# Norm statistics as four columns instead of a 128x512 tile, in a three-block transformer kernel

## The chip, the cores and the metric

One Trainium2 chip, one of its cores. The metric is the device time of one execution of the whole program, in microseconds (us). The core has five engines that run their own instruction streams and meet at semaphores: PE (TensorE, matrix products; PEld is its loading of weights), DVE (VectorE), ACT (ScalarE), POOL (GpSimd) and SP (SyncE, which here only starts transfers).

## The reference, cut to what matters

512 tokens of 2048 features go through two hybrid layers and then a second block. All norms divide by a root mean square over the features, one number per token:

```python
def rms_norm(x, w, eps=1e-6):
    return x * rsqrt(mean(x * x, axis=-1) + eps) * w

# layer l = 0, 1
proj = rms_norm(x, pre_w) @ w_in                  # norm x0, x1
qc   = rms_norm(c_q, q_norm_w) @ w_uq             # norm cq0, cq1 (512 features)
kvc  = rms_norm(c_kv, kv_norm_w) @ w_ukv          # norm ckv0, ckv1 (512 features)
x    = x + rms_norm(y @ w_out, post_w)            # norm post0, post1
# second block
h    = ... rmsnorm(x, norm_gain) @ w_in_2 ...     # norm x2
h    = h + (h @ w_out_2 part) + (p @ w_ple) * sigmoid(h @ w_ple_gate)
out  = rmsnorm(h, final_gain)                     # norm fin
```

That is ten norms. Everything is in float32.

## The kernel before

**Layout.** Activations lie feature-major: a tile `tiles[:, kt]` is 128 features by 512 tokens, and `kt` counts 16 of them. A number per token therefore runs along the free axis and must be the same in all 128 partitions before it can multiply a tile.

**Products.** A weight or activation is split into a high part (rounded to the type `fp32r`) and a low part, and a product is three matmuls of 128x512 (lines 1657 to 1659). Weights come in units of four 128x256 blocks through a ring of four slots: SP loads `w_raw` (L393), ACT casts it to `w_hi` (L531, in `split_one`) as soon as PE has finished with the slot, POOL subtracts to make `w_lo` in two halves (L518), and PE waits for `wlo_done`. One unit is 24 matmuls. PE's order is written out by hand: `plan_units` numbers the units and each engine's code walks through them. At `first_pairs` (the first eight units of a block that starts with a norm) PE takes tile after tile, 12 matmuls each, as `act_lo[:, kt]` becomes ready.

**A norm.** Squares are summed over tiles into one 128x512 tile. For x0, x1 and x2, ACT writes 16 squares into `wide` and DVE adds them at the end in four wide operations (`sum_squares`, L1089: 4096, 2048, 1024 and 512 columns). For cq and ckv DVE squares and adds (`square_sum`), for post and fin it does so in the loop that takes the products out of PSUM (L1315 to L1318, L1638 to L1642). PE multiplies the sum with a 128x128 matrix of ones (`ones_product`, L1726), which leaves the token's sum in all partitions, 128x512. `rms` (L937 to L939) then does on 128x512: scale and add eps on DVE, root on ACT (`root`, L557), reciprocal on DVE. For cq and ckv the result lies in `rstd_lat`, for the others in `rstd`. The norm of x is applied late: the products are taken from PSUM with a multiplication by `rstd` (L908). PE transposes `rstd` (L1881) and DVE copies four columns of it to `rcol` (L1196), which a later product needs per token.

**Where the norms stand on PE.** x0 and x1: the ones product after the second of four `ckr` units; the units of `ckv` that follow need PSUM banks that DVE frees by taking the first products with `rstd`. cq: after the third `ckv` unit. ckv: after the second unit of `bg1`. post0 and post1: after the last unit of `wo`; nothing is queued on PE until DVE has made the first tile of the next block (`tiles*rstd` L1330, gain and residual L1331, low part L916; ACT does high part L745 and square L747 between). x2: right after its `first_pairs`. fin: last; then 16 scaled tiles (L1647) and the stores (L504).

## Time and profile before

| | us |
|---|---|
| median of three runs | 2897.19 |
| lowest run | 2896.59 |
| the profiled execution, in all | 2892.89 |
| its span, first to last instruction | 2891.1 |
| PE busy (share of the span) | 2733.6 (95%) |
| DVE busy | 1514.5 (52%) |
| ACT busy | 848.4 (29%) |
| POOL busy | 1202.4 (42%) |

Times in the trace are microseconds from the start of the span; a row of the timeline gives start and length. Matmuls are pipelined: a row's length overlaps the next row's start, so the cost of one is the distance between starts. An `x2` behind a row merges two instructions; one float32 product is two of them on PE, one `fp32r` product is one. The clock column is the granted TensorE clock: 1.00 is 2.4 GHz, 0.50 is 1.2 GHz.

### The profile page before, as it was taken

How to read it: one execution, taken by the hardware profiler on the slowest of the kernel's cores; microseconds unless marked ns; L12 is line 12 of the kernel's file. 1: busy time of each engine (PE TensorE's matmuls, PEld its weight loads, DVE VectorE, ACT ScalarE, POOL GpSimd, SP SyncE). 2: the span in 40 equal slices, each digit the busy share in tenths (PEclk: the TensorE clock that was granted, in tenths of full speed). 3: DMA queues.
4: the chain of work that ended last, by engine and by line, in shares of the span. 5: the costliest groups of instructions: out<-in, count | busy, mean ns of one | idle time of the engine just before them, and what ended most of it. 6: DMA issues, size and time to landing. Idle time of an engine off the chain costs nothing.

```text
span 2891.1 us, 34107 instructions
## 1 busy us (share of the span) xinstructions
PE 2733.6 (95%) x12638; PEld 2152.5 (74%) x12638; DVE 1514.5 (52%) x2088; ACT 848.4 (29%) x1374; POOL 1202.4 (42%) x860
## 2 busy tenths in 40 slices
PE   7999999999998999999999999798999988999996
PEld 5777877877786787887777787676666667788885
DVE  4653146478425644227548732938898683211524
ACT  4233214225313332213315422312222233322321
POOL 5452442442443653343352344423332254455542
PEclk9999999999999999999999999898999989999998
DMA  4332332321433332232231333312211322432331
GB/s 153 97 116 66 95 89 61 89 77 45 167 94 97 118 105 81 87 95 73 71 90 52 142 101 98 140 59 80 66 51 59 124 80 85 151 98 89 108 95 73
DMA packets 246196, 268.65 MB, mean 93 GB/s; under 512 B 20544, under 2 KB 237248, under 8 KB 243648
## 3 DMA queue, kind: packets, MB, share of 16 engines
q1 hardware_dynamic: 240512, 222.33, 25.9%
q10 hardware_dynamic: 5568, 44.74, 4.0%
q8 instruction: 78, 1.28, 0.2%
q14 instruction: 38, 0.31, 0.0%
HBM read 246.06 MB, written 20.97 MB: 92 GB/s over the span
## 4 chain that ended last, share of the span: by engine, by line
issue 55%; POOL 31%; PE 12%; DVE 1%; POOLq 1%; ACT 0%; DVEq 0%
POOL w_lo L518 31%; PE gemm_ps L1657 4%; PE gemm_ps L1658 4%; PE gemm_ps L1659 4%; DVE tiles L1647 0%; POOLq L516 0%; POOLq L514 0%; PE to_ps L1658 0%; PE to_ps L1657 0%; PE s_ps L1658 0%; PE s_ps L1657 0%; PE s_ps L1659 0%; PE to_ps L1659 0%; DVE rstd L939 0%; PE to_ps L1726 0%
## 5 line engine op out<-in xcount | busy, mean ns | idle before, releaser
L518 POOL TENSOR_TENSOR w_lo<-w_raw,w_hi 128x512 fp32r<-128x512 f32 x856 | 1202.2, 1427 | 1644.7 <-ACT w_hi L531 1644.6
L1657 PE MATMUL gemm_ps<-act_hi,w_hi 128*128 128x512 f32 x2848 | 1142.7, 401 | 75.7 <-DVE mask_b L1099 21.2
L1658 PE MATMUL gemm_ps<-act_lo,w_hi 128*128 128x512 f32 x2848 | 1118.5, 393 | 0.0
L1659 PE MATMUL gemm_ps<-act_hi,w_lo 128*128 128x512 f32 x2848 | 1118.2, 393 | 0.0
L531 ACT CAST w_hi<-w_raw 128x1024 fp32r<-128x1024 f32 x428 | 447.9, 1050 | 1500.4 <-PE gemm_ps L1659 1308.9
L1657 PEld LDWEIGHTS gemm_ps<-act_hi,w_hi 128*128 128x128 f32 x2848 | 540.7, 190 | 224.4 <-issue 87.4
L1659 PEld LDWEIGHTS gemm_ps<-act_hi,w_lo 128*128 128x128 f32 x2848 | 540.3, 190 | 116.0
L1658 PEld LDWEIGHTS gemm_ps<-act_lo,w_hi 128*128 128x128 f32 x2848 | 541.1, 190 | 111.9 <-issue 4.3
L908 DVE TENSOR_TENSOR tiles<-gemm_ps,rstd 128x512 f32<-128x512 f32 (+1 forms) x58 | 39.3, 689 | 281.3 <-PE gemm_ps L1659 278.0
L1315 DVE COPY tiles<-gemm_ps 128x512 f32 x32 | 22.2, 693 | 221.1 <-PE gemm_ps L1659 220.7
L1608 DVE TENSOR_TENSOR tiles<-gemm_ps,att 128x512 f32<-128x512 f32 x16 | 11.0, 690 | 141.5 <-PE gemm_ps L1659 141.5
L984 DVE TENSOR_TENSOR att<-to_ps,sin_t 128x512 f32<-128x512 f32 x40 | 27.6, 689 | 79.9 <-PE to_ps L1754 79.9
L1022 DVE TENSOR_REDUCE small<-s_ps 128x1 f32<-128x128 f32 (+5 forms) x48 | 26.7, 557 | 81.0 <-PE s_ps L1798 80.6
L1638 DVE SCALAR_TENSOR_TENSOR att<-att 128x512 f32 x16 | 14.7, 919 | 101.8 <-ACT att L885 88.0
L584 ACT ACTIVATE att<-att,small 128x256 f32<-128x256 f32 (+1 forms) x128 | 60.1, 473 | 19.4 <-DVE small L1018 19.4
L1813 PE MATMUL to_ps<-cst,att 128*128 128x128 f32 x384 | 57.6, 272 | 6.8 <-ACT att L606 3.6
L1813 PEld LDWEIGHTS to_ps<-cst,att 128*128 128x128 f32 x384 | 46.5, 139 | 18.3 <-issue 4.4
L916 DVE SCALAR_TENSOR_TENSOR act_lo<-tiles,col,act_hi 128x512 fp32r<-128x512 f32 x48 | 45.8, 972 | 22.9 <-ACT act_hi L657 22.5
L1657 PE MATMUL gemm_ps<-sub_hi,w_hi 128*128 128x512 f32 x96 | 42.2, 439 | 14.7 <-DVE tiles L1507 14.4
L995 DVE TENSOR_TENSOR tiles<-tiles,att 128x512 f32<-128x512 f32 x36 | 54.0, 1500 | 1.2
L591 ACT ACTIVATE att<-s_ps,small 128x128 f32<-128x128 f32 (+1 forms) x64 | 31.8, 500 | 69.5 <-DVE small L1023 69.5
L908 DVE TENSOR_TENSOR att<-gemm_ps,rstd 128x512 f32<-128x512 f32 x32 | 21.6, 688 | 55.6 <-PE gemm_ps L1659 55.5
(380 smaller groups left out, 3166.8 us busy)
## 6 DMA issues: line engine op xcount, KB each, us to landing
w_raw<-in_w_in_dram SPq DMA_DIRECT2D x248, 512.0 KB
w_raw<-in_w_out_dram SPq DMA_DIRECT2D x96, 512.0 KB
w_raw<-in_w_ple_gate_dram SPq DMA_DIRECT2D x32, 512.0 KB
gate_scratch<-att ACTq DMA_DIRECT2D x16, 512.0 KB, 2.6
x_scratch<-tiles ACTq DMA_DIRECT2D x4, 2048.0 KB, 7.9
att<-x_scratch ACTq DMA_DIRECT2D x2, 4096.0 KB, 13.2
w_raw<-in_w_glu_dram SPq DMA_DIRECT2D x32, 256.0 KB
tiles<-in_x_dram ACTq DMA_DIRECT2D x4, 1024.0 KB, 10.7
```

The costliest lines, as they stand in the source:

```text
L518: ins = pool.tensor_tensor(w_lo[:, s, k:k + 2], w_raw[:, s, k:k + 2], w_hi[:, s, k:k + 2].bitcast(F32), ALU.subtract)
L531: act.copy(w_hi[:, slot], w_raw[:, slot]).then_inc(whi_done, 1)
L584: act.activation(v, v, ACT.Exp, bias=sm[:, 4 + j:5 + j], scale=SCALE[br], accum_out=sm[:, 8 + j:9 + j])
L591: last = act.activation(prob[n % 3][:, c * 512:c * 512 + nk], src, ACT.Exp, bias=sm[:, 4 + c:5 + c], scale=SCALE[br], accum_out=sm[:, 8 + ...
L908: tt(dst, ps[:, f, :], scale[:], ALU.mult).then_inc(bank_taken[f], 1)
L916: ins = stt(act_lo[:, kt], tiles[:, kt], scale, act_hi[:, kt].bitcast(F32), ALU.mult, ALU.subtract)
L984: tt(sq[:, n % 2], t_ps[:, n % 2, :], sin_t[:], ALU.mult).then_inc(rope_read, 1)
L995: tt(t, t, sq[:, n % 2], ALU.add).then_inc(roped, 1)
L1657: pe.matmul(ps, left_hi, right_hi, start=first, stop=False, skip_group_check=True)
L1658: pe.matmul(ps, left_hi, right_lo, start=False, stop=False, skip_group_check=True)
L1659: return pe.matmul(ps, left_lo, right_hi, start=False, stop=last, skip_group_check=True)
L1813: mm = pe.transpose(t_ps[:, a, k * 128:(k + 1) * 128], prob[n % 3][:, a * 512 + k * 128:a * 512 + (k + 1) * 128], ident)
```

## The change

**The statistic.** `ones_product` is replaced by two steps. `norm_cols` multiplies, for each of four token blocks, the 128x128 block of squares (as the weights) with four columns of ones: the sum comes out as a column, one token per partition. `rms` then does its arithmetic on 128x4 (L950 to L953), writes four 128x128 diagonals (L955), and `norm_rows` (L1764) multiplies ones with the 128x512 of diagonals, which gives the row form in PSUM, read from there by who needs it; for x norms it is copied to `rstd` (L959). The transposes of `rstd` and the copy to `rcol` go.

**The sums of squares.** `sum_squares` is replaced by `partial_sum`: 11 additions of 128x512, one after most tiles, which leave five partial sums (tiles 0, 4, 8, 12 and 15) that `norm_cols` adds up in PSUM. For post and fin the last two tiles are squared on ACT instead of DVE, straight from PSUM at post, and enter as two more partial sums.

**Casts.** L531 becomes two casts of 128x512, each with its semaphore step, and POOL waits for each half.

**Moves.** The products for lambda stand at the start instead of behind the sine tables; ACT casts two units fewer ahead of the roots of x0 and x1.

```diff
-                act.copy(w_hi[:, slot], w_raw[:, slot]).then_inc(whi_done, 1)
+                for k in range(0, UK, 2):
+                    act.copy(w_hi[:, slot, k:k + 2], w_raw[:, slot, k:k + 2]).then_inc(whi_done, 1)
...
-            split_until(14)
+            split_until(12)
             root("x0")
...
                 through(("wo", l), 32)
+                for f in range(2):
+                    act.wait_ge(mm_done, unit_end(("wo", l), 31) + f + 1)
+                    if f:
+                        act.wait_ge(ssq_in, NORMS[f"post{l}"] + 1)
+                    act.activation(last_sqs[f], gemm_ps[:, f, :], ACT.Square).then_inc(last_sq, 1)
                 root(f"post{l}")
...
             def rms(norm, n_feat):
-                to = rstd_lat if norm[0] == "c" else rstd[:]
-                dve.wait_ge(ssq_out, SSQ[norm])
-                ts(to, o_ps[:, 0, :], 1.0 / n_feat, EPS, ALU.mult, ALU.add).then_inc(var_done, 1)
-                dve.wait_ge(sqrt_done, NORMS[norm] + 1)
-                dve.reciprocal(to, to).then_inc(rstd_done, 1)
-                dve.wait_ge(rstd_done, NORMS[norm] + 1)
+                i, c = NORMS[norm], norm_col(norm)
+                dve.wait_ge(ssq_out, i + 1)
+                ts(c, o_ps[:, 0, 0:16].rearrange("p (t n) -> p t n", n=4)[:, :, 0], 1.0 / n_feat, EPS,
+                   ALU.mult, ALU.add).then_inc(var_done, 1)
+                dve.wait_ge(sqrt_done, i + 1)
+                own.link(dve.reciprocal(c, c))
+                for t in range(TT):
+                    ins = ts(diag[:, t * 128:(t + 1) * 128], ident, norm_col(norm, t, 1), None, ALU.mult)
+                ins.then_inc(diag_done, 1)
+                dve.wait_ge(rows_done, i + 1)
+                if norm[0] == "x":
+                    dve.tensor_copy(rstd[:], o_ps[:, 0, :]).then_inc(rstd_done, 1)
+                    dve.wait_ge(rstd_done, int(norm[1:]) + 1)
...
-            def sum_squares(v):
-                dve.wait_ge(sq_done, KT * (v + 1))
-                for n in (8, 4, 2, 1):
-                    ins = tt(wide_flat[:, 0:n * T], wide_flat[:, 0:n * T], wide_flat[:, n * T:2 * n * T], ALU.add)
+            def partial_sum(v, kt):
+                if kt % 4 and kt < KT - 1:
+                    dve.wait_ge(sq_done, KT * v + kt + 1)
+                    ins = tt(wide[:, kt - kt % 4], wide[:, kt - kt % 4], wide[:, kt], ALU.add)
...
-            def ones_product(norm, squares=sq[:, 0]):
-                pe.wait_ge(ssq_in, SSQ[norm])
-                pe.matmul(o_ps[:, 0, :], ones[:], squares, start=True, stop=True).then_inc(ssq_out, 1)
+            def norm_cols(norm, squares):
+                pe.wait_ge(ssq_in, NORMS[norm] + 1)
+                for t in range(TT):
+                    for i, s in enumerate(squares):
+                        mm = pe.matmul(o_ps[:, 0, 4 * t:4 * t + 4], s[:, t * 128:(t + 1) * 128], ones[:, 0:4],
+                                       start=i == 0, stop=i == len(squares) - 1)
+                mm.then_inc(ssq_out, 1)
+            def norm_rows(norm):
+                pe.wait_ge(diag_done, NORMS[norm] + 1)
+                pe.matmul(o_ps[:, 0, :], ones[:], diag, start=True, stop=True).then_inc(rows_done, 1)
+            def x_cols(v):
+                pe.wait_ge(sq_done, KT * (v + 1))
+                norm_cols(f"x{v}", [wide[:, k] for k in (0, 4, 8, 12, 15)])
...
                 first_pairs(("cq", l), f"x{l}")
+                x_cols(l)
...
-                    if j == 1:
-                        ones_product(f"x{l}", wide[:, 0])
+                    if j == 0:
+                        norm_rows(f"x{l}")
...
                 one_pair(("ckv", l), 1, 0)
-                pe.wait_ge(rstd_done, NORMS[f"x{l}"] + 1)
-                for t in range(TT):
-                    mm = pe.transpose(t_ps[:, 0, t * 128:(t + 1) * 128], rstd[:, t * 128:(t + 1) * 128], ident)
-                mm.then_inc(rcol_tp, 1)
+                norm_rows(f"cq{l}")
```

Not shown: cq's columns stand where its ones product stood; ckv's too, with its rows one unit later; post, x2 and fin have columns and rows next to each other.

**PE after the first eight units of a layer, x0.** Before, the ones product came 24 matmuls into `ckr` (the fragment shows its neighbours):

```order
L1659 MATMUL to_ps<-act_hi,w_lo 128x512
L1726 MATMUL to_ps<-att,ones 128x512
L1657 MATMUL to_ps<-act_hi,w_hi 128x512
```

Of the change, the seam between `first_pairs` (s_ps) and the first `ckr` unit (to_ps), cut after its third matmul:

```order
L1687 MATMUL s_ps<-act_hi,w_lo 128x512
L1757 MATMUL to_ps<-ones,att 128x4 x20
L1685 MATMUL to_ps<-act_hi,w_hi 128x512
L1686 MATMUL to_ps<-act_lo,w_hi 128x512
L1687 MATMUL to_ps<-act_hi,w_lo 128x512
```

One product became 20 with 128 weights and four columns each, ahead of the unit, and the rows (L1764) follow 12 matmuls later.

**DVE after the norm post0.** These rows make the tiles of layer 1; before, three per tile:

```order
L1330 TENSOR_TENSOR tiles<-tiles,rstd 128x512
L1331 SCALAR_TENSOR_TENSOR tiles<-tiles,col,att 128x512
L916 SCALAR_TENSOR_TENSOR act_lo<-tiles,col,act_hi 128x512
L1330 TENSOR_TENSOR tiles<-tiles,rstd 128x512
L1331 SCALAR_TENSOR_TENSOR tiles<-tiles,col,att 128x512
L916 SCALAR_TENSOR_TENSOR act_lo<-tiles,col,act_hi 128x512
```

Of the change, from the fourth tile on:

```order
L1352 TENSOR_TENSOR tiles<-tiles,to_ps 128x512
L1353 SCALAR_TENSOR_TENSOR tiles<-tiles,col,att 128x512
L929 SCALAR_TENSOR_TENSOR act_lo<-tiles,col,act_hi 128x512
L1109 TENSOR_TENSOR att<-att 128x512
L1352 TENSOR_TENSOR tiles<-tiles,to_ps 128x512
L1353 SCALAR_TENSOR_TENSOR tiles<-tiles,col,att 128x512
L929 SCALAR_TENSOR_TENSOR act_lo<-tiles,col,act_hi 128x512
```

The additions L1109 that stood behind the last tile as four wide ones stand between the tiles now.

## Rows read from the trace of the kernel before

**Rows 1.** Timeline, PE: start us, length us, engine, line, operation, count, [idle before <-releaser]

```profile
72.65 1.02 PE L1726 MATMUL to_ps<-att,ones 128*128 128x512 f32 x2
...
73.75 0.40 PE L1658 MATMUL to_ps<-act_lo,w_hi 128*128 128x512 f32 x1
...
80.16 0.47 PE L1657 MATMUL gemm_ps<-act_hi,w_hi 128*128 128x512 f32 x1 [1.03 <-POOL w_lo L518]
...
108.14 0.40 PE L1659 MATMUL gemm_ps<-act_hi,w_lo 128*128 128x512 f32 x1
108.37 0.60 PE L1881 MATMUL to_ps<-cst,rstd 128*128 128x128 f32 x4
108.73 0.48 PE L1657 MATMUL gemm_ps<-act_hi,w_hi 128*128 128x512 f32 x1
```

**Rows 2.** Timeline around norm post0, PE and DVE

```profile
909.41 1.15 PE L1726 MATMUL to_ps<-att,ones 128*128 128x512 f32 x2 [3.50 <-DVEq L1324]
...
911.98 3.35 DVE L939 RECIPROCAL rstd<-rstd 128x512 f32<-128x512 f32 x1 [0.69 <-ACT rstd L557]
...
915.37 0.69 DVE L1330 TENSOR_TENSOR tiles<-tiles,rstd 128x512 f32<-128x512 f32 x1
...
919.05 0.77 PE L1657 MATMUL gemm_ps<-act_hi,w_hi 128*128 128x512 f32 x1 [8.49 <-DVE act_lo L916]
```

**Rows 3.** Stretch table, PE: busy (count), granted clock, DMA share, GB/s

```profile
912.00:914.00 2.00, 0.00 (x0) 0.50 0.68 236
```

**Rows 4.** Timeline through the tiles of x1, and norm x1: DVE and PE

```profile
933.18 1.79 DVE L1330 TENSOR_TENSOR tiles<-tiles,rstd 128x512 f32<-128x512 f32 x1
...
956.80 11.64 DVE L1089 TENSOR_TENSOR att<-att 128x4096 f32<-128x4096 f32 x4
...
964.78 0.39 PE L1659 MATMUL s_ps<-act_hi,w_lo 128*128 128x512 f32 x1
...
981.51 1.29 DVE L908 TENSOR_TENSOR tiles<-gemm_ps,rstd 128x512 f32<-128x512 f32 x2 [3.14 <-DMA x_scratch<-tiles]
...
982.34 0.76 PE L1657 MATMUL gemm_ps<-act_hi,w_hi 128*128 128x512 f32 x1 [3.37 <-DVE tiles L908]
```

**Rows 5.** Timeline, norm x2 on PE

```profile
1862.62 2.02 PE L1726 MATMUL to_ps<-att,ones 128*128 128x512 f32 x2 [3.26 <-DVE att L1089]
1871.49 0.76 PE L1657 MATMUL gemm_ps<-act_hi,w_hi 128*128 128x512 f32 x1 [6.84 <-DVE tiles L908]
```

**Rows 6.** Timeline, norm fin: PE and DVE

```profile
2869.41 1.89 PE L1726 MATMUL to_ps<-cos_t,ones 128*128 128x512 f32 x2 [4.40 <-DVEq L1644]
...
2876.12 10.69 DVE L1647 SCALAR_TENSOR_TENSOR tiles<-tiles,col,rstd 128x512 f32<-128x512 f32 x16
```

**Rows 7.** Timeline at the lambda product: PEld, PE, DVE

```profile
130.75 0.50 PEld L1888 LDWEIGHTS to_ps<-col,ones 64*128 64x128 f32 x2 [5.85 <-DVE col L1119]
130.75 0.59 PE L1888 MATMUL to_ps<-col,ones 64*128 64x4 f32 x2 [5.43 <-DVE col L1119]
...
130.83 1.27 DVE L908 TENSOR_TENSOR tiles<-gemm_ps,rstd 128x512 f32<-128x512 f32 x2
...
131.65 0.77 PE L1657 MATMUL gemm_ps<-sub_hi,w_hi 128*128 128x512 f32 x1 [0.31 <-DVE tiles L908]
```

**Rows 8.** By line, L2000: min/median/max ns, first and last start us

```profile
L2000 PE MATMUL to_ps<-att,tiles x128: 196/196/217, 1936.7 to 1938.0; 128*32 128x32 f32 x128
```

**Rows 9.** Timeline, first matmul, norm cq0 and a small copy, PE and DVE

```profile
21.18 0.77 PE L1657 MATMUL gemm_ps<-act_hi,w_hi 128*128 128x512 f32 x1 [21.18 <-DVE mask_b L1099]
...
108.50 1.42 DVE L947 SCALAR_TENSOR_TENSOR tiles<-tiles,col,att 128x512 f32<-128x512 f32 x2
...
113.86 0.16 DVE L1196 COPY col<-to_ps 128x4 f32<-128x4 f32 x1
```

**Rows 10.** Page, costliest groups: xcount | busy us, mean ns | idle before, releaser

```profile
L518 POOL TENSOR_TENSOR w_lo<-w_raw,w_hi 128x512 fp32r<-128x512 f32 x856 | 1202.2, 1427 | 1644.7 <-ACT w_hi L531 1644.6
L531 ACT CAST w_hi<-w_raw 128x1024 fp32r<-128x1024 f32 x428 | 447.9, 1050 | 1500.4 <-PE gemm_ps L1659 1308.9
```

More of the change, by code:

```diff
@@ L338, in build_program @@
         NORMS = {k: i for i, k in enumerate(order)}
+        last_sqs = [rstd[:], sq[:, 1]]
         VERS, total = {}, 0
@@ L344, in build_program, with norm_col @@
             total += n_tiles
-        SSQ = {"x0": 1, "cq0": 2, "ckv0": 3, "post0": 4, "x1": 5, "cq1": 6, "ckv1": 7, "post1": 8, "x2": 9, "fin": 10}
+        def norm_col(norm, t=0, n=4):
+            return C("rcol" if norm[0] == "x" else "ncol", t, n)
         def unit_end(key, units):
@@ L555, in root @@
                 act.wait_ge(var_done, NORMS[norm] + 1)
-                to = rstd_lat if norm[0] == "c" else rstd[:]
-                act.activation(to, to, ACT.Sqrt).then_inc(sqrt_done, 1)
+                act.activation(norm_col(norm), norm_col(norm), ACT.Sqrt).then_inc(sqrt_done, 1)
             def split_act(version, kt, src, scale):
@@ L889, in _ @@
                 act.activation(sq[:, f], gemm_ps[:, f, :], ACT.Tanh, scale=0.5).then_inc(bank_taken[f], 1)
+            for f in range(2):
+                act.wait_ge(fin_in, f + 1)
+                act.activation((rstd, sin_t)[f][:], tiles[:, 14 + f], ACT.Square).then_inc(last_sq, 1)
             root("fin")
@@ L946, in latent @@
                     if kt < 4:
-                        stt(tiles[:, first + kt], tiles[:, first + kt], C(gain, 4 * l + kt), rstd_lat,
+                        stt(tiles[:, first + kt], tiles[:, first + kt], C(gain, 4 * l + kt), o_ps[:, 0, :],
                             ALU.mult, ALU.mult).then_inc(lat_in, 1)
@@ L1093, in sum_squares @@
                         ins.then_inc(ssq_in, 1)
-            for kt in range(KT):
+            tt(C("prod", 0, 2)[0:64], C("lam4", 0, 2)[0:64], C("lam4", 2, 2)[0:64], ALU.mult)
+            tt(C("prod", 2, 2)[0:64], C("lam4", 4, 2)[0:64], C("lam4", 6, 2)[0:64], ALU.mult).then_inc(lam_sum, 1)
+            for kt in range(KT + 1):
                 if kt == 4:
@@ L1308, in _ @@
                 own.link(dve.memset(sq[:, 0], 0.0))
-                for first, count in ((0, 2), (2, 2), (4, 4)):
+                for first, count in ((0, 2), (2, 2), (4, 3)):
                     with dve.Fori(0, count) as i:
@@ L1324, in _ @@
                 dve.nop().then_inc(ssq_in, 1)
+                for f in range(2):
+                    dve.wait_ge(last_sq, 2 * l + f + 1)
+                    take(f, tiles[:, 14 + f], None)
                 rms(f"post{l}", D)
@@ L1329, in _ @@
                     if kt < KT:
-                        own.link(tt(tiles[:, kt], tiles[:, kt], rstd[:], ALU.mult))
+                        if kt >= 14:
+                            dve.wait_ge(bank_taken[kt % 2], at[("wo", l)][1] + 9)
+                        own.link(tt(tiles[:, kt], tiles[:, kt], o_ps[:, 0, :], ALU.mult))
                         stt(tiles[:, kt], tiles[:, kt], C("post", 16 * l + kt), wide[:, kt],
@@ L1642, in _ @@
                     own.link(tt(cos_t[:], cos_t[:], sin_t[:], ALU.add))
-            own.leave(8)
+            own.leave(7)
             dve.nop().then_inc(ssq_in, 1)
+            for f in range(2):
+                w, t = wide[:, 14 + f], tiles[:, 14 + f]
+                dve.wait_ge(bank_taken[f], 7 + (at[("pleg", 0)][1] + 2))
+                stt(w, sq[:, f], 1.0, w, ALU.add, ALU.mult).then_inc(pleg_tanh, 1)
+                dve.wait_ge(pleg_tanh, 14 + f + 3)
+                stt(t, w, 0.5, t, ALU.mult, ALU.add).then_inc(fin_in, 1)
             rms("fin", D)
             for kt in range(KT):
-                stt(tiles[:, kt], tiles[:, kt], C("fgain", kt), rstd[:], ALU.mult, ALU.mult).then_inc(fin_scaled, 1)
+                stt(tiles[:, kt], tiles[:, kt], C("fgain", kt), o_ps[:, 0, :], ALU.mult, ALU.mult).then_inc(fin_scaled, 1)
         @block.tensor
@@ L1902, in _ @@
                     if j == 1:
-                        ones_product(f"ckv{l}")
+                        norm_cols(f"ckv{l}", [sq[:, 0]])
+                    elif j == 2:
+                        norm_rows(f"ckv{l}")
                 if l:
@@ L1974, in _ @@
                 pairs(("wo", l), 8, first=1, order=Y_UNITS)
-                ones_product(f"post{l}")
+                pe.wait_ge(last_sq, 2 * l + 2)
+                norm_cols(f"post{l}", [sq[:, 0]] + last_sqs)
+                norm_rows(f"post{l}")
             first_pairs(("si", 0), f"x{LAYERS}")
-            ones_product(f"x{LAYERS}", wide[:, 0])
+            x_cols(LAYERS)
+            norm_rows(f"x{LAYERS}")
             def state_rows(v):
@@ L2106, in _ @@
             pairs(("pleg", 0), 8, first=1)
-            ones_product("fin", cos_t[:])
+            pe.wait_ge(last_sq, 2 * LAYERS + 2)
+            norm_cols("fin", [cos_t[:], rstd[:], sin_t[:]])
+            norm_rows("fin")
 _INS = ["x", "positions", "w_in", "w_uq", "w_ukv", "w_out", "p_2", "w_in_2", "w_pool_2", "w_glu_2", "w_out_2",
```

49 lines of the change are left out of this document (22 added, 27 removed).

## The prediction

> **What bounds the kernel now.** I read the page first: PE is busy for 95% of the span, so time comes only from what PE executes and from the 157 us in which it stands still. Then I followed its stops along the timeline; those that a norm causes are few. The reader is to see, in this order: after post0 PE stops for 3.50 us, does the ones product and stops for 8.49 us, of which the reciprocal alone is 3.35 [rows 2]; the same pattern returns at post1. At x2 it stops for 3.26 and 6.84 us [rows 5], at x1 for 3.37 us, behind DVE which waited for the store of x [rows 4], at x0 for 1.03 us [rows 1], and at fin 4.40 us before the ones product, with the output scaled only from 2876.12 on [rows 6]. The lambda product is released 5.43 us late, but the unit behind it also needs the banks that DVE frees at 130.83, so that stop ends with DVE's queue and not with the product [rows 7]. Everywhere else PE is fed: cq0, cq1, ckv0 and ckv1 lie almost wholly under weight units.
>
> So the change can win only at post0, post1, x2 and fin. At x0, x1, cq and ckv it adds work to an engine that is full.
>
> **The price of a column product.** The trace has no float32 product of 128 weight columns with four moving ones, except the lambda product (64 rows): two instructions, weight loads of 0.50 us together, matmuls of 0.59 us together, at half clock [rows 7]. From lengths and ends the two loads start 0.17 us apart, the two matmuls 0.22. At full clock that is 0.085 to 0.11 us for an instruction. A float32 block with 128 moving columns fits it: four transposes take 0.36 us, 0.09 each [rows 1]. Bound below: 128 instructions with 32 weight columns each start within 1.3 us, 0.011 each [rows 8]; bound above: 0.22, half clock [rows 7]. I take 0.09, since the form is that of rows 7. The change has three norms x with 20 products, three (post, fin) with 12 and four (cq, ckv) with 4: 112 products, 224 instructions, 20.2 us of PE time. A whole ones product costs 0.87 us at full clock (72.65 to 73.75 less one matmul of 0.23, the distance of 108.14 to 108.37) and some 2.0 us at half clock [rows 1, 5]; rows cost the same.
>
> Here a page speaks against my price. The Trainium skill, TensorE: Matmul & The Clock Gate, section Back-to-back issue gap, gives about 60 cycles, 25 ns, for a matmul with 1 to 64 moving columns. By that the 224 would be an estimated 5.6 us. No row here has this form at full clock, so the page is not refuted; the sum below stands on rows 7.
>
> **The small steps.** Between columns and diagonals stand a scale, a root, a reciprocal and four diagonals of 128x128. A copy of 128x4 out of PSUM took 0.16 us [rows 9]; seven such steps and the hops between engines make 1.5 us, where 128x512 took 0.69 + 0.63 + 3.35 and hops. The root's table load stays ahead of its wait at x0 and lies under the column products at post and fin: nothing.
>
> **Term by term, plus is slower.**
>
> Start: the first matmul waits for `mask_b` [rows 9]; now the sums of tiles 1 and 2 stand ahead of it on DVE, 0.7 us each, half of one covered. +0.9. PE has no stop behind it that would absorb it until x0.
>
> x0: 40 x 0.09 = 3.6 for the columns; rows for the ones product, even; the stop of 1.03 goes, since `rstd` is ready earlier than `ckv` begins. +2.6.
>
> cq0: rows are queued behind the unit that ended at 108.37. They end 1.05 later, 109.4, where DVE began the latents at 108.50 [rows 1, 9]: +0.9. Columns 8 x 0.09 = 0.7 for 0.87: -0.15. The lambda operations and the copy to `rcol` leave DVE's queue: -0.2. All of it passes through the sine tables into the take at 130.83. +0.6.
>
> ckv0: columns -0.15, rows +0.87. +0.7.
>
> post0 and x1: the last matmul ends at 905.92 (909.41 less 3.50). ACT does a cast (1.05, now in halves [rows 10]) and two squares of about 0.55: 908.2. Columns 24 x 0.09 and drain: 910.6. Small steps: 912.1. The clock is at 0.50 by 912 [rows 3], so rows take 2.0: DVE starts the tiles at 914.1 instead of 915.37. But each tile then costs DVE more. Before, nine tiles took 17.8 us, 2.05 each after the first, and while POOL runs an operation takes 1.79 instead of 0.69 [rows 4], twice for four operations, 8.7 us in all. Low part 12 now comes at 914.1 + 3.5 + 12 x 2.05 + 8 sums x 0.73 + 8.7 = 956.7, later than PE would want it, and PE has four tiles of 2.72 left: 967.6, where it ended its first pairs at 965.0. Then columns 3.6, rows 0.9, four `ckr` units 10.9: 983.0. Before, PE went on at 982.34, after a stop that left it at half clock (0.76 for a matmul that is 0.40 long otherwise), some 1.3 us for the first six: 983.6 [rows 4]. The four wide sums of 11.64 us vanish, but PE never waited for their end here. The store of x is issued two casts earlier and no longer ends last. -0.6.
>
> cq1 and ckv1: as in layer 0, but rows are now on PE's path and the transposes (0.36 [rows 1]) go: +0.35 and +0.7. +1.0.
>
> post1 and x2: the first pairs end 2.7 later, as at x1: 1862.05. Columns 3.8 with drain, small steps 1.5, rows at half clock 2.0, copy to `rstd` 0.7, first take 0.8: 1870.8 against 1871.49 [rows 5]. -0.7.
>
> fin: last matmul 2865.01. Two tanh, two DVE steps of 0.75, square: 2868.0. Columns 2.4, small steps 1.5, rows 1.9: scaling starts at 2873.8 instead of 2876.12 [rows 6]. -2.3. The 10.69 us behind it read PSUM instead of SBUF, at the same length as other products out of PSUM (L908, 0.64 each in a pair [rows 4]).
>
> Halved casts: POOL gets its first half 0.5 us earlier, and ACT pays an instruction more per unit. PE waits for neither: a unit lasts 5.4 us, POOL needs 2.85 of it and is released by ACT, ACT by PE [rows 10]. 0, cover 2.5 us per unit.
>
> Sum: 0.9 + 2.6 + 0.6 + 0.7 - 0.6 + 1.0 - 0.7 - 2.3 = +2.2 us on the profiled execution of 2892.89: 2895.1. The median of the runs stands 4.3 above that execution, so the forecast for a median is 2899.
>
> **The rivals.**
>
> *Columns are cheap.* If the weight loads hide behind each other, an instruction costs 0.05 or less. Speaks for it: rows 8. Against: those are quarter-width tiles. At 0.05 the sum is 2.2 - 224 x 0.04 = -6.8, median 2890; at the page's 25 ns (same section of the Trainium skill) it would be an estimated 2885. At the bound of rows 8, -15.6: 2881.5.
>
> *The columns leave the clock low* (the other side, slower). Products of four columns hardly fill the array, and the clock was at 0.50 after a stretch with little more than a ones product in it [rows 3]. If it falls during x0's and x1's columns too, these double (3.6 each, also at x2), rows cost 1.1 more and the next dozen matmuls pay 0.2 each: about +6 at each of two sites and +3.6 at x2, +16 in all: 2915. It decides from the point where one x norm shows a clock below 0.7 in the 5 us after its columns. Against it: the ones product among the weight units of x0 left the matmul at 73.75 at its 0.40 [rows 1], and a column stretch is not much longer.
>
> *DVE becomes the bound in the first pairs.* Margin per tile: 2.72 for PE, 2.05 + 0.55 for DVE. If the added sums meet POOL more often than the old ones, each pays 1.1 more; five of them per x norm, two norms: +11, 2910. For it: every DVE operation beside POOL is stretched [rows 4].
>
> *The halves starve the ring.* Needs 2.5 us more per unit; 0.14 us for each of 428 units would already be 58 us, 2%. Nothing in rows 10 points there.
>
> **How the numbers follow.** Forecast 0.45, its own range 2895 to 2904 (0.08 to 0.11 per instruction, start and cq0 half a microsecond either way). Cheap columns 0.22, 2882 to 2894. Low clock 0.13, 2905 to 2916. DVE bound 0.17, 2904 to 2912. Others 0.03. Range for 8 in 10: 2888 to 2910; the bound above for the price, +29 us, would need half clock everywhere and is left out. A measurement of this kernel tells 2% (58 us) from no change, and no case but the last reaches it: faster 0.01, same 0.98, slower 0.01.
>
> **What would show each step.** Distance between column products 0.09 us, x columns 3.6 us long. No stop before `ckv` at x0 and x1. First pairs of x1 and si ending 48 to 50 us after the diagonals' use begins, with PE stopping for DVE between tiles 8 and 12. Reciprocals no longer above 0.2 us. Scaling at fin starting 8.8 us after the last `pleg` matmul, 11.1 before. The forecast is wrong if the columns cost under 0.06 or over 0.12, or if the clock at x0 falls.

## The result, and the profile after

The changed kernel takes 2902.01 us, the median of 20 runs (2897.18 to 2907.39), where the kernel before took 2894.16 us in 20 runs beside it. The ratio is 1.0027 with a 95% interval of 1.0021 to 1.0033, so 7.8 us (6 to 10) slower, and within 2%. One of the 20 runs of the kernel before, at 5244.23 us, stands far off the others; without it their median would be 2893.41. I had forecast +2.2 us, and 2899 on a base of 2897.19 us. The profiled executions exaggerate the difference. The one of the kernel before (2892.89 us) stands 1.3 us below its median and the one of the changed kernel (2906.21 us) 4.2 above its own, so that the spans, 2891.1 and 2904.4 us, differ by 13.3.

Part 1 of the page after, the busy time, share and instructions of each engine:

```profile
PE 2765.3 (95%) x12854; PEld 2182.2 (75%) x12854; DVE 1475.0 (51%) x2138; ACT 885.7 (30%) x1808; POOL 1183.9 (41%) x860
```

The first matmul, from PE's timeline (start and length in us, engine, line, operation, out<-in; in brackets the idle time ahead and what ended it), and DVE's timeline just before it. It answers the 21.18 of [rows 9]:

```profile
24.50 0.77 PE L1685 MATMUL gemm_ps<-act_hi,w_hi 128*128 128x512 f32 x1 [24.50 <-DVE mask_b L1121]
...
19.90 0.68 DVE L1109 TENSOR_TENSOR att<-att 128x512 f32<-128x512 f32 x1
...
21.29 0.68 DVE L1109 TENSOR_TENSOR att<-att 128x512 f32<-128x512 f32 x1
22.01 1.17 DVE L1120 CAST ident_b<-cst 128x128 bf16<-128x128 f32 x1
23.10 1.30 DVE L1121 CAST mask_b<-cst 128x128 bf16<-128x128 f32 x1
```

Two sums of 0.68 us stand ahead of the casts, and the casts, which now fall beside POOL's work, are 1.17 and 1.30 long instead of 0.21. That second part I had not counted.

The norm x0 on PE, columns (L1757) and rows (L1764), and on DVE scale, reciprocal, diagonals and copy (answering [rows 1]):

```profile
69.81 6.14 PE L1757 MATMUL to_ps<-ones,att 128*128 128x4 f32 x40
75.81 0.78 PE L1685 MATMUL to_ps<-act_hi,w_hi 128*128 128x512 f32 x1
76.39 0.63 PE L1686 MATMUL to_ps<-act_lo,w_hi 128*128 128x512 f32 x1
...
80.24 1.02 PE L1764 MATMUL to_ps<-att,ones 128*128 128x512 f32 x2
...
75.99 0.16 DVE L950 TENSOR_SCALAR col<-to_ps 128x4 f32<-128x4 f32 x1 [29.75 <-PE to_ps L1757]
76.42 0.18 DVE L953 RECIPROCAL col<-col 128x4 f32<-128x4 f32 x1 [0.27 <-ACT col L562]
76.64 0.87 DVE L955 TENSOR_SCALAR att<-cst,col 128x128 f32<-128x128 f32 x4
81.30 0.69 DVE L959 COPY rstd<-to_ps 128x512 f32<-128x512 f32 x1 [3.79 <-PE to_ps L1764]
```

And PE's table by stretches of x0 (busy us and instructions, granted clock, DMA share, GB/s), the third stretch being the first matmuls behind the columns; below them the 5 us behind the columns of x0, x1 and x2:

```profile
69.80:72.40 2.60, 2.60 (x25) 1.00 0.02 6
72.40:75.80 3.40, 3.40 (x18) 0.50 0.57 159
75.80:79.20 3.40, 3.40 (x9) 0.50 0.79 189
79.20:82.00 2.80, 2.80 (x11) 0.99 0.14 46
...
75.80:80.80 5.00, 5.00 (x16) 0.65 0.62 154
979.20:984.20 5.00, 5.00 (x17) 0.66 0.99 300
1874.20:1879.20 5.00, 2.08 (x2) 0.50 1.02 321
```

The first 24 column instructions start 0.111 us apart. Then the granted clock falls to 0.50 (1.2 GHz, from 2.4) although PE never stands still, the rest start 0.213 apart, and the eight matmuls behind them are 0.54 to 0.78 long instead of 0.39. At x2 the clock fell in the kernel before too, as its ones product began, behind a stop of 3.26 us [rows 5].

The norm post0 (answering [rows 2]), first and last row of the 24 column instructions, rows, and restart; and the end of fin (answering [rows 6]):

```profile
916.45 0.38 PE L1757 MATMUL to_ps<-ones,att 128*128 128x4 f32 x2 [2.21 <-ACT att L750]
...
918.93 0.57 PE L1757 MATMUL to_ps<-ones,att 128*128 128x4 f32 x2
921.11 2.07 PE L1764 MATMUL to_ps<-att,ones 128*128 128x512 f32 x2 [1.61 <-DVE att L955]
926.89 0.77 PE L1685 MATMUL gemm_ps<-act_hi,w_hi 128*128 128x512 f32 x1 [3.71 <-DVE act_lo L929]
...
2889.49 10.62 DVE L1675 SCALAR_TENSOR_TENSOR tiles<-tiles,col,to_ps 128x512 f32<-128x512 f32 x16 [2.17 <-PE to_ps L1764]
```

**Where the time went.** I cut PE's timeline at the same places in each trace: ends of first pairs, the start of `ckv`, the restart at uq0 (the first weight unit that needs the norm cq0), the last matmul of `wo` (a layer's output product, ahead of post) and of `pleg` (the last product, ahead of fin). The second block starts at its unit `si`. "Again" is a second trace of the changed kernel. Lengths in us:

| stretch | before | after | again | forecast | found |
|---|---|---|---|---|---|
| to the first matmul, and x0's first pairs | 67.20 | 69.81 | 70.47 | +0.9 | +2.6, +3.3 |
| x0: columns, rows, `ckr` | 12.95 | 19.47 | 19.49 | +2.6 | +6.5 |
| cq0: `ckv` to uq0's restart | 51.49 | 52.33 | 52.33 | +0.6 | +0.8 |
| ckv0 and the attention of layer 0 | 774.27 | 772.64 | 770.75 | +0.7 | -1.6, -3.5 |
| post0 | 13.13 | 12.65 | 13.68 | | |
| first pairs of x1 | 45.96 | 47.91 | 47.90 | | |
| x1 to `ckv`; with the two above | 17.33 | 17.88 | 19.48 | -0.6 | +2.0, +4.6 |
| cq1, ckv1 and the attention of layer 1 | 817.73 | 815.23 | 815.18 | +1.0 | -2.5 |
| post1, first pairs, x2 | 71.40 | 72.74 | 72.88 | -0.7 | +1.3, +1.5 |
| second block, si to fin | 993.53 | 999.16 | 998.96 | 0 | +5.6, +5.4 |
| fin to the end | 26.08 | 24.59 | 24.79 | -2.3 | -1.5, -1.3 |

The same cut by kind of time, up to PE's last instruction: PE's idle time, half of the busy time at a granted clock of 0.50, and the rest, which is work at full clock:

| kernel | idle | lost to the clock | work |
|---|---|---|---|
| before | 137.7 | 46.1 | 2687.5 |
| changed | 124.2 | 57.1 | 2708.2 |
| changed, again | 127.4 | 54.3 | 2709.3 |
| one summed tile (e1) | 136.8 | 47.3 | 2700.1 |
| and diagonals on ACT (e6) | 133.4 | 48.1 | 2699.0 |
| new scheme at post and fin alone (e8) | 122.0 | 52.5 | 2692.9 |
| and the store of x first (e9) | 118.1 | 56.7 | 2693.8 |

So the change does what it says: 13.5 us of stops are gone. It pays 20.7 us of PE work for them, and another 11.0 us at half clock. The second trace has 10.3, 21.8 and 8.2: the work is the same within about 1 us, the split between stops and clock is not. The row of e9 is that kernel's slowest run (2885.46 us, where its median is 2878.18).

### The profile page after: what moved, and what is told of

Its sections match the earlier page's. It is cut to its first block and busy times, and to the rows that moved or that the text cites. A ratio compares the mean times of both kernels' runs of the same rounds, so it can differ in the third digit from the quotient of the medians.

```text
span 2904.4 us, 35445 instructions
## 1 busy us (share of the span) xinstructions
PE 2765.3 (95%) x12854; PEld 2182.2 (75%) x12854; DVE 1475.0 (51%) x2138; ACT 885.7 (30%) x1808; POOL 1183.9 (41%) x860
## 5 line engine op out<-in xcount | busy, mean ns | idle before, releaser
L524 POOL TENSOR_TENSOR w_lo<-w_raw,w_hi 128x512 fp32r<-128x512 f32 x856 | 1183.7, 1406 | 1677.9 <-ACT w_hi L537 1677.8
L537 ACT CAST w_hi<-w_raw 128x512 fp32r<-128x512 f32 x856 | 486.0, 618 | 1480.5 <-PE gemm_ps L1687 1289.0
L921 DVE TENSOR_TENSOR tiles<-gemm_ps,rstd 128x512 f32<-128x512 f32 (+1 forms) x58 | 39.3, 688 | 285.0 <-PE gemm_ps L1687 284.8
L919 DVE COPY tiles<-gemm_ps 128x512 f32<-128x512 f32 x24 | 16.1, 682 | 70.5 <-ACT rstd L750 38.4
```

Source lines behind the costliest of these rows:

```text
L524: ins = pool.tensor_tensor(w_lo[:, s, k], w_raw[:, s, k], w_hi[:, s, k].bitcast(F32), ALU.subtract)
L537: act.copy(w_hi[:, slot, k:k + 2], w_raw[:, slot, k:k + 2]).then_inc(whi_done, 1)
L921: tt(dst, ps[:, f, :], scale[:], ALU.mult).then_inc(bank_taken[f], 1)
```

## The experiments

Ratios are those to the kernel before on the same chip; the changed kernel's was 1.0027, and 1.0030 (1.0018 to 1.0043) when it was run again. The intervals are about 2.5 to 3.8 us wide to either side, which bounds what a single comparison can settle. One microsecond is 0.00035.

**One summed tile (e1).** Is it the number of columns?

```
-                if kt % 4 and kt < KT - 1:
+                if kt:
...
-                    ins = tt(wide[:, kt - kt % 4], wide[:, kt - kt % 4], wide[:, kt], ALU.add)
+                    ins = tt(wide[:, 0], wide[:, 0], wide[:, kt], ALU.add)
...
-                norm_cols(f"x{v}", [wide[:, k] for k in (0, 4, 8, 12, 15)])
+                norm_cols(f"x{v}", [wide[:, 0]])
```

> DVE adds all sixteen squares of x0, x1 and x2 into one tile (15 additions instead of 11), so that each x norm has 4 column products (8 instructions) instead of 20 (40). Theory 'the columns and the clock that they lose': in the changed kernel the 40 instructions take 6.0, 4.4 and 5.9 us at x0, x1 and x2, 0.111 each at full clock and 0.213 at half, and 7 to 8 ckr matmuls behind them are 0.2 us longer each. With 8 instructions the clock stays at full: -5.1 -1.6 at x0, -3.5 -1.6 at x1, -5.0 +0.7 (one more addition behind the last square) at x2, about -16 us: 2886. Theory 'only the instructions count' (the clock falls anyhow): 96 x 0.111 to 0.15, -10.7 to -14 us less nothing. Rival 'DVE is the bound in the first pairs': four more additions of 0.73 to 1.8 us per x norm are late for the last low parts, so PE's stop of 1.1 us for act_lo at x1 and x2 grows by 3 to 7 us each: gain only 2 to 9 us, 2893 to 2900.

Measured: 1.0031 (1.0018 to 1.0044), no gain. The timelines at x1 of PE, DVE and POOL:

```profile
976.38 0.95 PE L1758 MATMUL to_ps<-ones,att 128*128 128x4 f32 x8
982.99 1.12 PE L1765 MATMUL to_ps<-att,ones 128*128 128x512 f32 x2 [2.78 <-DVE att L955]
...
977.37 0.16 DVE L950 TENSOR_SCALAR col<-to_ps 128x4 f32<-128x4 f32 x1 [1.84 <-PE to_ps L1758]
977.92 0.18 DVE L953 RECIPROCAL col<-col 128x4 f32<-128x4 f32 x1 [0.38 <-ACT col L562]
978.13 4.81 DVE L955 TENSOR_SCALAR att<-cst,col 128x128 f32<-128x128 f32 x4
...
974.94 9.22 POOL L524 TENSOR_TENSOR w_lo<-w_raw,w_hi 128x512 fp32r<-128x512 f32 x7
```

POOL at x0 in the changed kernel, whose diagonals stand at 76.64 to 77.51:

```profile
73.08 1.26 POOL L524 TENSOR_TENSOR w_lo<-w_raw,w_hi 128x512 fp32r<-128x512 f32 x1
```

The eight columns take 0.95 us as expected, and 8 us of work and 10 us of lost clock are gone (7 against the second trace). But the idle time rose by 12.6: the four diagonals take 4.81 us instead of 0.87, and PE waits 3.42, 2.78 and 5.63 us for them at x0, x1 and x2. No theory had this. In the changed kernel POOL ended at 74.34 and had nothing further until the diagonals were done. That the long columns had kept PE from freeing weight slots is my reading of it; what the traces show is that behind short columns the diagonals run beside POOL. At x0 the clock fell in e1 as well, at 77.3 us behind that stop, so that x0 took 19.31 us against 19.47. And the first pairs of x1 and x2 took 49.4 us instead of 47.9: the four more sums per norm do come late, as the third theory had it, for 1.5 us each.

**Diagonals on ACT (e6).** Tests just that; everything else is as in e1.

```
                 act.activation(norm_col(norm), norm_col(norm), ACT.Sqrt).then_inc(sqrt_done, 1)
+                act.wait_ge(recip_done, NORMS[norm] + 1)
+                for t in range(TT):
+                    ins = act.activation(diag[:, t * 128:(t + 1) * 128], ident, ACT.Copy, scale=norm_col(norm, t, 1))
+                ins.then_inc(diag_done, 1)
```

> As the kernel with one tile (e1), and ACT writes the four diagonals (Copy with the column as its scale) instead of DVE, at every norm. Theory 'DVE's diagonals beside POOL ate the gain of e1': there PE waited 3.4, 2.8 and 5.6 us for them at x0, x1 and x2, the four of them being 4.8 to 5.3 us long. On ACT they take about 4 x 0.25 us, whatever POOL does: the stops fall by 3.4, 2.8 and 3.7 us, one hop of 0.1 us more at post and fin: -9 to -10 us against e1, 2891. Rival 'ACT is as slow beside POOL or stands behind casts': the stops stay, within 2 us of e1. Rival 'the sums are late, not the diagonals' (one accumulating tile): the wait moves to the columns.

Measured: 1.0010 (0.9999 to 1.0021), 6 us below e1 against 9 to 10 expected. Of the stop for the rows 0.65 us are left at x0 and nothing at x1; x0 takes 13.66 us (19.31 in e1) and x1 12.72 (15.76). At x2, ACT's timeline, then DVE's:

```profile
1863.12 0.40 ACT L565 ACTIVATE att<-cst,col 128x128 f32<-128x128 f32 x1 [0.24 <-DVE col L957]
...
1863.43 0.97 ACT L565 ACTIVATE att<-cst,col 128x128 f32<-128x128 f32 x3
...
1869.88 1.29 DVE L925 TENSOR_TENSOR tiles<-gemm_ps,rstd 128x512 f32<-128x512 f32 x2 [3.43 <-DMA x_scratch<-tiles]
```

The diagonals take 1.3 us, although POOL is busy from 1859.97 to 1866.61, and at x2 the gain runs into the next wait: DVE's takes (the products taken out of PSUM times `rstd`) stand behind the store of x. The theory holds; the missing microseconds are this wait, and 998.6 us in the second block where e1's trace had 994.5.

**The start (e2).**

```
-                if kt:
+                if kt == 4:
+                    for k in range(3):
+                        partial_sum(0, k)
+                if kt >= 4:
                     partial_sum(0, kt - 1)
```

(and the two lambda products back in the sine tables)

> Only the start is undone: the two lambda products stand again in the sine tables, and the sums of tiles 1 to 3 of x0 come behind the copy to mask_b. Theory 'start': the first matmul waited until 24.5 us for mask_b (21.2 before); it starts 2.7 to 3.3 us earlier and all of that stays to the end, since PE has no stop until the first pairs are done: -2.5 to -3.3 us, 2899. Rival 'the start is absorbed': PE then waits for low parts or weights within the first pairs instead, first pairs end at the same time, 0: 2902. Rival 'it was the transfer': the first matmul stays at 24 us since params or the constants arrive late: 0.

Measured: 1.0037 (1.0024 to 1.0050). The first matmul starts at 21.78 instead of 24.50, and PE is ahead of the changed kernel by 2.3 us at the end of x0 and by 4.0 at the end of layer 0's `wo` (3.0 and 2.8 against its second trace). Behind it all of that is lost. The attention of layer 1 took 817.5 us (815.2 in both traces of the changed kernel) and post1 14.49 (12.44 in both); x1 took 19.48 (17.88), but that it did in the second trace of the changed kernel too. The first theory is right on the start and not seen in the sum.

**Whole casts (e3).**

> Only the casts of the weights are whole again (one ACT instruction and one signal per unit). Theory 'halves cost nothing' (the prediction): 0 +-1 us, 2902; the stages from 1963 to 2334 us take as long as in the changed kernel (370 us). Rival 'the halves crowd ACT in the state stage': there PE stood 13.5 us for DVE's queue, against 11.3 before, and the stage from the low part at the POOL stop to the stop at its end took 357 us instead of 353: with whole casts it falls back to 353 and the whole to -4 us, 2898. Rival 'the halves help at the boundaries' (the first half of w_lo is there earlier): +1 to +3 us.

```
-                for k in range(0, UK, 2):
-                    act.copy(w_hi[:, slot, k:k + 2], w_raw[:, slot, k:k + 2]).then_inc(whi_done, 1)
+                act.copy(w_hi[:, slot], w_raw[:, slot]).then_inc(whi_done, 1)
```

Measured: 1.0036 (1.0023 to 1.0049); the halves cost nothing that can be told from zero and may save 2 us. The trace has the second block at 995.7 us, 3.5 less than the changed kernel's, but the first matmul at 25.28, x1's first pairs at 49.7 us (47.9), and PE 7 us behind at si (6 against the second trace).

**The latents as before (e4).** One ones product each for cq and ckv.

```
-                        norm_cols(f"cq{l}", [sq[:, 0]])
+                        ones_product(f"cq{l}")
                 one_pair(("ckv", l), 1, 0)
-                norm_rows(f"cq{l}")
```

(likewise at ckv, with root and reciprocal of 128x512)

> Only the four latent norms (cq, ckv of both layers) go back to one ones product and a root and reciprocal of 128x512. Theory 'PE is full there': 8 column instructions at 0.11 and rows of 0.87 for one ones product of 0.87 make 0.9 us per norm; at cq0 0.6 and at cq1, ckv0, ckv1 0.9 each fall away: -3.3 us, 2899. Rival 'the latents are on time only by the new way': the reciprocal of 3.35 us comes back into DVE's queue, and PE's stop before uq0 (6.49 us now) grows by 3 to 4 us, with one at ukv: +3 to +6 us. Rival 'neither': within 1 us.

Measured: 1.0007 (0.9998 to 1.0016), about 6 us below the changed kernel. PE's work falls from 45.83 to 44.88 us in the stretch of cq0, by 1.1 in that of ckv0 and from 806.5 to 804.9 in layer 1, in all 3.6 us, and the long reciprocals do not come back as a stop (6.32 us at uq0, 6.49 before the edit). The rest is the second block, 991.4 us here, where no norm product was edited. No run shows why; more on it stands below.

**The columns spread (e5).** The same 40 instructions, ten behind each k step of the first `ckr` unit.

```
+                        if j == 0:
+                            for i, q in enumerate((0, 4, 8, 12, 15)):
+                                mc = pe.matmul(o_ps[:, 0, 4 * k:4 * k + 4], wide[:, q, k * 128:(k + 1) * 128],
+                                               ones[:, 0:4], start=i == 0, stop=i == 4)
```

> At x0 and x1 the 40 column instructions no longer stand in one stretch: ten of them follow each of the first four k steps of the first ckr unit, and the rows stand behind the second unit instead of the first. Theory 'the dense stretch lets the clock fall': in the changed kernel the clock fell to 0.50 2.6 us into the columns of x0 and just behind those of x1. Spread out, it stays at 1.00, the 40 instructions cost 4.4 us, and x0 falls by 1.7 (columns) and 1.6 (matmuls behind them), x1 by 1.6: -5 us if nothing else. Rival 'the same number of small products lowers the clock anyhow': it falls within the first unit, 0. Rival 'diagonals beside POOL': in the kernel with one tile DVE's four diagonals took 1.3 us each beside POOL instead of 0.2; here they come while POOL fills the ring, 4.7 us instead of 0.9, and PE stops 1 to 3 us for the rows: the gain is halved, -2 us or nothing.

Measured: 1.0030 (1.0019 to 1.0042), no change. PE's stretches at x0, columns first:

```profile
69.70:75.30 5.60, 5.60 (x41) 1.00 0.37 97
75.30:82.20 6.90, 6.90 (x23) 0.51 0.39 114
```

The clock fell at x0 all the same, a little later, and 3.4 us were lost as before; at x1 it held at 1.00 with the same instructions, and the stretch was 16.39 us instead of 17.88. My theory of the dense stretch falls for x0. What tells x0 from x1 here no run shows.

**Moving columns (e11).** `ones[:, 0:32]` in place of `ones[:, 0:4]`.

> The changed kernel with 32 moving columns in each column product instead of 4 (the reciprocal still reads one of them). Theory 'the weight load sets the price': an instruction with 128 float32 weight columns stays at 0.111 us at full clock, 6.0 to 6.1 us for the 40 of x0, and the time is the changed kernel's. Rival 'the moving columns do': 28 more columns in each of 224 instructions make them at least 0.012 us longer each at 2.4 GHz with one column a cycle, 0.123, 0.5 us more per x norm; with four cycles a float32 column, 0.047 more, 1.9 us per x norm, 10 us in all.

One run: 2905.82 us. The 40 of x0 take, in PE's timeline,

```profile
71.16 5.11 PE L1757 MATMUL to_ps<-ones,att 128*128 128x32 f32 x40
```

less than the 5.76 and 6.14 us of the changed kernel's two traces, because the clock fell later; at full clock the starts stay 0.11 us apart. Eight times the moving columns cost nothing. That leaves the weight load as the price, which no run changed by itself.

**The changed kernel again (e10).**

> The changed kernel once more, word for word, for its second trace. Theory 'the second block's +5.6 us (999.2 instead of 993.5 us from the restart at si to the last matmul of fin) is one execution's timing of the clock': eight kernels with the same instructions there gave 991.4 to 999.4, so a second trace gives another value in that range, and the median 2898 to 2900 beside 2890.5 (ratio 1.0027 to 1.0035). Rival 'the change causes it' (casts in halves or what the first blocks leave behind): again 998 to 1000. The x0 norm, whose cost theory puts on the columns and the clock, must come out the same: 19.4 to 19.6 us from the end of the first pairs to ckv.

Measured: 1.0030. x0 took 19.49 us, as expected. The second block took 998.96 us, as in the first trace (999.16), so its length belongs to this kernel and not to one execution: the first theory falls.

**A combination (e7)**: e6 with e4's latents and an early `mask_b`.

> e6 with the latent norms of the kernel before (one ones product each, as e4) and with mask_b ahead of the sums of x0's tiles 1 to 3. If the effects add: e4 measured 0.9980 of the changed kernel's ratio, -6 us, the start -2 to -3 us, e6 another -9: 16 us below the changed kernel, 0.9970 of the kernel before, 2882 beside 2890.9. If the start gives nothing (as the run of it suggests, since the clock's phase at x1 took it back): 2885. If neither e6's nor e4's gains add: as the kernel before.

Measured: 0.9992 (0.9983 to 1.0001), 2888.0 beside 2890.5. Of the 16 us below the changed kernel that the sum of all three would give, 10 to 11 came. Without the start, which had shown nothing in its own run, the gains add to within 3 us. This still has the sums tile by tile, which make first pairs 3.4 us longer (49.4 against 46.0 at x1).

**The new scheme at post0, post1 and fin alone (e8)**, all else as in the kernel before.

```
+                if norm in NEW:
+                    c = norm_col()
...
-                ones_product(f"post{l}")
+                pe.wait_ge(last_sq, 2 * l + 2)
+                norm_cols(f"post{l}", [sq[:, 0]] + last_sqs)
+                norm_rows(f"post{l}")
```

> The kernel before with the new scheme at post0, post1 and fin alone (columns, diagonals, rows, last squares on ACT); the x norms, the latents, the sums of squares and the casts as before. Theory 'the change wins only there': the stop between last matmul and restart was 13.1 us at each post, 12.65 in the changed kernel, and fin's end 26.1 us, now 24.6: -0.5 -0.5 -1.5 = -2.5 us (my prediction put it at 1.3 per post and 2.3 at fin, -4.9), 2888.5 beside 2890.9. Rival 'low clock behind the small products takes it back': 0 +-1. Rival 'the extra DVE work of two late tiles moves the first pairs of x1': + 1.

Measured: 0.9976 (0.9966 to 0.9986), 6.9 us faster than the kernel before, where 2.5 were expected. The trace is 8.8 us shorter: 1.0 at fin, 0.6 at post1, 1.7 at x1 and 1.9 at x2, each with its first pairs, 4.1 in the two attentions and 1.0 in the second block, where nothing was edited; post0 itself took 14.79 us against 13.13, since its columns ran at half clock (5.3 us instead of 3.05). So at the three norms that the edit touches this trace gains nothing in sum, and the gain is found behind them. DVE at x1:

```profile
972.43 3.35 DVE L967 RECIPROCAL rstd<-rstd 128x512 f32<-128x512 f32 x1 [0.70 <-ACT rstd L565]
979.60 1.29 DVE L924 TENSOR_TENSOR tiles<-gemm_ps,rstd 128x512 f32<-128x512 f32 x2 [3.82 <-DMA x_scratch<-tiles]
```

The take stands 3.8 us behind the store again, as in e6.

**The store of x first (e9 on e8, e12 on the kernel before).**

```
+                    if kt % 8 == 7:
+                        act.dma_start(x_dram[:, kt - 7:kt + 1, :], tiles[:, kt - 7:kt + 1, :]).then_inc(x_out, 16)
                     if kt % 4 == 3 and kt > 4:
                         split_until(...)
-                    if kt % 8 == 7:
-                        act.dma_start(x_dram[:, kt - 7:kt + 1, :], tiles[:, kt - 7:kt + 1, :]).then_inc(x_out, 16)
```

> The kernel with the new scheme at post0, post1 and fin alone (e8), and at x1 and x2 ACT issues each store of x before the weight casts that stood ahead of it. In e8 the store's second half was issued at 970.3 at x1 and 1854.9 at x2, and DVE's takes waited for its landing until 979.6 and 1862.6, 3.8 and 1.9 us after the reciprocal. Theory 'the store ends last': it is now issued about 955 and 1847, lands before the reciprocal, and x1 and x2 are 2.9 and 1.9 us shorter: -4.8 us against e8, 2879.5 beside 2890.5. Rival 'the store crowds the weights': 2 MB more between the weight loads delay the first pairs by as much: 0. Rival 'DVE is late anyhow': the takes start less than 1 us earlier, -1 us.

> The kernel before with one edit: at x1 and x2 ACT issues each store of x ahead of the weight casts. There, DVE's takes at x1 began 3.1 us after its reciprocal, behind the landing of the store (issued at 973.4 us), and at x2 directly behind the reciprocal. Theory 'the effects add': x1 becomes 3.1 us shorter, x2 stays: ratio 0.9989 of the kernel before, 2888.8 beside 2891.9; then the store is worth 3 us alone, post and fin 7 alone, and 10 to 15 together. Rival 'the store's gain was e9's alone, since only the new posts let DVE finish early': 0, 1.0000. Rival 'most of e9's 14.8 us is the store': 0.997 or below.

Measured: e9 0.9949 (0.9935 to 0.9962), 2878.2 us, the fastest here; e12 0.9973 (0.9963 to 0.9983). DVE at x1 in e9:

```profile
973.36 3.35 DVE L967 RECIPROCAL rstd<-rstd 128x512 f32<-128x512 f32 x1 [0.70 <-ACT rstd L565]
976.75 1.29 DVE L924 TENSOR_TENSOR tiles<-gemm_ps,rstd 128x512 f32<-128x512 f32 x2
```

The wait is gone. x1 is 12.12 us (15.91 in e8), x2 8.61 (9.88); in e12 x1 is 14.25 (17.33), 3.1 us less, exactly the wait removed. Yet e12's median fell by 7.8 us, more than the 3.1 that its theory had and just short of the last rival's 0.997. In its trace 5.7 us come from two stretches that the edit does not touch: layer 0's attention 771.3 us (774.3) and layer 1's 815.0 (817.7). The medians add up: 6.9 for e8 and 7.8 for e12 against 14.8 for e9.

## Why the prediction was right in its class and wrong in its terms

**The time** came out 7.8 us above the kernel before, in the range, 5.6 above the forecast's +2.2. "About even, a little slower" was right, and so was the mechanism: wins at post, x2 and fin against added work where PE is full. But that the total came so near is in part luck. Added up over start, x0, cq0, x1, x2 and fin, the trace has some +12 us (+15 in the second) where I had +0.5. The two attentions gave 4.1 back (6.1 in the second) where I had +1.7, and the rest of the distance to 7.8 us is that the profiled executions exaggerate.

**The price of a column product** was mis-sized: 0.111 us at full clock and 0.213 at half, where I took 0.09 from [rows 7], whose own distances gave 0.085 to 0.11. The right reading was there: the matmul starts of [rows 7] were 0.22 apart at half clock, which makes 0.11 at full clock, and I averaged them with the 0.17 of the loads. The four transposes of [rows 1] say the same: their starts stand 0.109 us apart in the trace, and my 0.09 came from dividing the 0.36 to the next matmul's start by four. 224 x 0.021 is 4.7 us. The Trainium skill, which I had cited for its rule on the gap between matmuls, has a nearer one: TensorE: Matmul & The Clock Gate, section LDWEIGHTS (loading the stationary operand), puts a load at its number of weight columns over 1.2 in ns, whatever the rows, an estimated 107 ns for 128. The trace's 0.111 at full clock agrees, and e11 shows that the moving columns don't count. The 25 ns of the section that I cited is shown by no row here.

**The clock at x0** is the step that failed, and the prediction had named its fall as a sign of being wrong. I gave it 13%; by the criterion that I gave (below 0.7 in the 5 us behind the columns) it fell at all three: 0.65, 0.66, 0.50, though at x2 it had fallen before the change too. What I argued against it, a ones product among weight units that kept its clock [rows 1], was one product of 0.9 us, not 4.4. The stretch of x0 became 6.5 us longer: +4.1 of work, +3.4 of clock, less the stop of 1.0. That rival's +16 was too much, though: it doubled whole column stretches and added six microseconds at each of two sites, and the traces have 3.4 us at x0 and 1.7 or 3.4 at x1. At x2 the columns took 5.9 us, 1.5 more than at full clock, not 3.6. What makes the clock fall under the columns stays open: e5 shows that it is not only their standing in one block.

**Start.** +0.9 forecast, +2.6 and +3.3 found. I counted the sums ahead of `mask_b` and not that the two casts behind them would then meet POOL, 2.5 us for what had been 0.4.

**cq0** was right: +0.6 forecast, +0.8 found. ckv0, cq1 and ckv1 can't be read from their stretches, but e4 shows the price of the four in PE work, 3.6 us where I had 2.3: rows of 0.87 are four times 0.87 and the columns save nothing against a ones product (8 x 0.111 = 0.89).

**post0 and x1.** The order of events came as told: rows at half clock (2.07 us), tiles starting 9.0 us behind the last matmul (8.2 forecast, 9.45 before), one stop for DVE of 1.14 us between the late tiles, no stop before `ckv`. I had the first pairs end 2.6 us later than before, counted from the last `wo` matmul; they ended 1.5 later in one trace and 2.5 in the other. The miss is again the columns of x1 (4.4 instead of 3.6) and the 1.7 to 3.4 us of clock. The rival *DVE bound* did not come: first pairs became 1.9 us longer at x1 and at x2, less than the 2.7 of the forecast itself, where it needed 5.5 more.

**fin.** -1.5 instead of -2.3: scaling starts 9.66 us behind the last matmul, where I had 8.8. The last squares were there 2.80 us behind that matmul (3.0 forecast); the columns took 3.1 instead of 2.4 us.

**The halved casts** cost nothing (e3), as forecast.

**The second block**, +5.6 us where nothing but the casts changed, is in no term. It is no accident of one execution (e10). Ten traces with its code (e3's but for the casts) gave 991.4 (e4, e7), 994.5, 994.6 (e1, e5), 995.7 (e3, whole casts) and 998.6 to 999.4 us (changed, again, e2, e6, e11). Four with the code of the kernel before gave 993.5, 992.6 (e8), 996.5 (e9) and 994.9 (e12). PE's work in it is 912.2 to 912.9 us in all fourteen, so no instruction of PE is the cause: what differs is idle time (44.7 to 53.2 us) and clock lost (29.3 to 39.3).

One place where they part is the clock some 28 us behind the restart at si, where PE stops for 3.2 us in every trace. In PE's stretches from 1900 to 1920 us of the changed kernel and of e4:

```profile
1900.00:1920.00 20.00, 16.80 (x70) 0.83 0.20 62
```

```profile
1900.00:1920.00 20.00, 16.79 (x83) 1.00 0.25 79
```

The five near 999 us all lost clock here, and so did e3 and e5, for e5 half as long; e1, e4 and e7 did not, and were some 2 us ahead after 400 weight matmuls (136.6 to 136.8 us behind the restart, 139.0 in the changed kernel). But that does not explain the +5.6. The kernel before lost clock here too, for 3.4 us, and was at 138.7; the changed kernel fell behind it only later (412.2 against 403.6 after 1000 weight matmuls). And e8 lost as much clock here as the changed kernel and was the shortest of its four, while e12 lost none and took 994.9. That the moment of arrival at such stops decides on the clock, and the clock on what DVE and PE wait for later, is a guess that these traces do not bear out as it stands, and no run shifted the arrival alone. The cause stays open, for the second block as for layer 0's attention (770.8 to 774.3 us) and layer 1's (812.0 to 817.7), and so does how much of the 7.8 us, and of e8's, e12's and e4's gains, is of this kind.

## What to carry to other kernels

On an engine that is 95% busy, replacing one wide product by many narrow ones can pay only where the engine stands still anyway. Here fin became 0.8 to 1.5 us shorter in every trace with the new scheme, and post anything from 0.8 us shorter to 1.7 longer. The new scheme at post and fin alone gave 0.9976, and 0.9949 with the store moved ahead of the casts, where the whole change gave 1.0027; how much of the 0.9976 the edited norms themselves earn is not shown. Read the price of a small product from the distance between starts, not from its moving columns, and price what the clock does behind it. When a wait is removed, look at once for the next one in the same place: behind the columns stood the diagonals beside POOL, behind the diagonals the store.

## What the runs showed of the hardware

- PE need not stand still for its clock to fall: 2.6 us into 40 back-to-back instructions of four moving columns the granted clock went from 1.00 to 0.50 at x0. With ten of them behind each of four k steps it fell at x0 and held at x1 (e5); with eight in all it held at both (e6).
- An instruction with 128 float32 weight columns and 4 moving ones costs 0.111 us at full clock and 0.213 at half, and the same with 32 (e11).
- A DVE `tensor_scalar` of 128x128 from SBUF took 0.2 us from start to start, and 1.2 to 1.3 beside POOL's subtractions (e1), six times as long; ACT's copy with a scale took 0.29 to 0.40, beside POOL too (e6). The Trainium skill, GPSIMD Engine Reference, section Specifications, says that GpSimd shares its SBUF interfaces with VectorE and that instructions in a two-port mode or with two SBUF inputs contend. The 1.79 us of a two-input product beside POOL, instead of 0.69 [rows 2, 4], agree. That the `tensor_scalar` of e1's 4.81 us is one of the first kind no run here shows.
- Stretches with the same instructions differed by 2 to 8 us between kernels that differ only elsewhere, while two traces of the changed kernel agreed to 0.2 us in the second block and were 1.9 us apart in layer 0's attention. A gain of a few microseconds at one site can't be read from a total.
